# Scan of a bidirectional RWKV-7 layer: both directions' triangular inverses kept in one 64x64 matrix, one factor of each level masked by GpSimd and one by VectorE

## What is computed

```
def step(S, inp):
    r_t, w_t, k_t, v_t, a_t, b_t = inp
    sa = jnp.einsum('zbhvk,zbhk->zbhv', S, a_t)
    S = S * w_t[..., None, :] + sa[..., :, None] * b_t[..., None, :] + v_t[..., :, None] * k_t[..., None, :]
    return S, jnp.einsum('zbhvk,zbhk->zbhv', S, r_t)
_, ys = lax.scan(step, jnp.zeros((2, B, H, N, N), f32), xs)
```

## Time and profile before

| | |
|---|---|
| median of 3 runs | 1307.17 us (1306.04 to 1310.15) |
| the profiled execution's own time | 1311.54 us |
| its span in the trace | 1309.7 us |
| TensorE busy | 96% of the span |
| VectorE, ScalarE, GpSimd busy | 71%, 49%, 34% |
| the scan's eight tiles | from 851.7 us to about 1069 us |

### The profile page before, as it was taken

The page is one execution under the profiler, slowest core; times in us unless marked ns, Lnnn a source line. Parts: engine busy times, 40 slices in busy tenths (PEclk is TensorE's granted clock), DMA queues, the critical chain, the costliest instruction groups (busy, mean ns, idle before and its releaser), DMA issues.

```text
span 1309.7 us, 30302 instructions
## 1 busy us (share of the span) xinstructions
PE 1252.8 (96%) x12608; PEld 1133.1 (87%) x12608; DVE 930.7 (71%) x1334; ACT 645.1 (49%) x1045; POOL 445.1 (34%) x228
## 2 busy tenths in 40 slices
PE   7999999999899999999999799989999998899998
PEld 5799999877889999889999699889989887799998
DVE  7677767686867776766677797686777657766554
ACT  5544446553544455654444466643444333555443
POOL 1244442212134444333444100173343512344442
PEclk9999999999999999999999799899999999999999
DMA  8344555422444555645445444110000014455442
GB/s 342 131 175 181 187 192 182 156 98 97 148 169 179 182 188 192 220 166 187 177 178 184 152 175 152 50 51 4 4 4 4 3 51 157 181 193 188 180 178 111
DMA packets 18667, 188.18 MB, mean 144 GB/s; under 512 B 2064, under 2 KB 2576, under 8 KB 3600
## 3 DMA queue, kind: packets, MB, share of 16 engines
q1 hardware_dynamic: 18576, 186.84, 39.1%
HBM read 185.78 MB, written 1.05 MB: 143 GB/s over the span
## 4 chain that ended last, share of the span: by engine, by line
PE 79%; DVE 13%; ACT 5%; issue 2%; DMA 1%; SPq 0%; DVEq 0%; ACTq 0%
PE gu_bank L257 22%; PE gu_bank L259 11%; PE bank L1382 7%; PE bank L236 7%; PE bank L238 7%; PE bank L237 7%; PE gu_bank L1401 5%; PE gu_bank L236 3%; PE gu_bank L238 3%; PE gu_bank L237 3%; DVE WL L193 2%; PE gu_bank L1382 2%; ACT WH L186 2%; DVE XSQ L407 1%; DVE HX L383 1%
## 5 line engine op out<-in xcount | busy, mean ns | idle before, releaser
L202 POOL TENSOR_TENSOR WL<-raw,WH 128x1024 fp32r<-128x1024 f32 x102 | 341.7, 3351 | 595.8 <-ACT WH L187 574.4
L257 PE MATMUL gu_bank<-HX,WH 128*128 128x512 f32 x1408 | 507.6, 402 | 15.0 <-DVE WL L193 12.4
L259 PE MATMUL gu_bank<-HX,WL 128*128 128x256 f32 x1408 | 397.3, 282 | 0.0
L193 DVE TENSOR_TENSOR WL<-raw,WH 128x2048 fp32r<-128x2048 f32 (+1 forms) x114 | 252.5, 2215 | 135.9 <-ACT WH L186 135.9
L257 PEld LDWEIGHTS gu_bank<-HX,WH 128*128 128x128 f32 x1408 | 266.8, 190 | 81.0 <-DVE WL L193 8.1
L259 PEld LDWEIGHTS gu_bank<-HX,WL 128*128 128x128 f32 x1408 | 268.4, 191 | 0.1
L186 ACT ACTIVATE WH<-raw 128x2048 fp32r<-128x2048 f32 (+1 forms) x114 | 204.6, 1795 | 25.6 <-PE gu_bank L238 13.5
L236 PE MATMUL bank<-PH,WH 128*128 128x256 f32 (+1 forms) x720 | 201.7, 284 | 1.0 <-ACT arena L1939 1.0
L237 PE MATMUL bank<-PL,WH 128*128 128x256 f32 (+1 forms) x720 | 201.6, 283 | 0.0
L238 PE MATMUL bank<-PH,WL 128*128 128x256 f32 (+1 forms) x720 | 201.6, 283 | 0.0
L438 ACT ACTIVATE work<-work 128x256 f32<-128x256 f32 x88 | 36.8, 418 | 279.3 <-DVE work L490 279.3
(11 more groups left out here) (310 smaller groups left out, 1970.5 us busy)
## 6 DMA issues: line engine op xcount, KB each, us to landing
raw<-stream_in SPq DMA_DIRECT2D x114, 1536.0 KB, 6.6
cst<-const_in SPq DMA_DIRECT2D x1, 1568.0 KB, 17.9
X<-xT_in SPq DMA_DIRECT2D x1, 1024.0 KB, 6.1
raw<-stream_in SPq DMA_DIRECT2D x1, 1024.0 KB, 8.1
arena<-hconst_in SPq DMA_DIRECT2D x2, 512.0 KB, 11.5
out<-X SPq DMA_DIRECT2D x4, 256.0 KB, 2.3
arena<-hconst_in SPq DMA_DIRECT2D x1, 768.0 KB, 14.6
arena<-fw_in SPq DMA_DIRECT2D x1, 512.0 KB, 8.9
```

The source lines that it names most:

```text
L193: nc.vector.tensor_tensor(WL[:, slot, :cut], raw[:, slot, :cut], WH[:, slot, :cut].bitcast(fp32), ALU.subtract).then_inc(lo_ready, 1)
L202: (eng or nc.gpsimd).tensor_tensor(WL[:, slot, cut:end], raw[:, slot, cut:end], WH[:, slot, cut:end].bitcast(fp32), ALU.subtract).then_inc ...
L257: nc.tensor.matmul(out[:, :], WH[:, slot, w:w + P], HX[:, x, :, :].rearrange("p i t -> p (i t)"), start=k == 0, stop=False)
L259: return nc.tensor.matmul(out[:, L:2 * L], WL[:, slot, w:w + P], HH[:, x, :], start=False, stop=k == CT - 1)
```

## The change

For each chunk one matrix `SQ` holds z=0's inverse below its diagonal and z=1's above it; the unit diagonal is common. Of the diagonal blocks of width b, the mask `tri` keeps the lower triangle where the block's index is even and the upper one where it is odd. Each level is done once for both directions on full 64x64 matrices: one `zee` and one `update` of 4 calls of `heads`, one copy by ScalarE, one addition by VectorE. For that both factors of a level are first masked: VectorE multiplies `SQ` by `tri` into `VQ` (for `zee`), and GpSimd multiplies the transposed `SW` by `tri` into `WQ` (for `update`). The matrix `GM` with both directions' entries is made by one copy of ScalarE and one predicated copy of VectorE; GpSimd masks it once a level, not twice. At the end VectorE separates the directions into `QF` with two masks, and ScalarE's two copies into `QF` go. The memsets of `ZB` go. TensorE's calls in a level are written in another order.

```diff
-            for z in range(2):
-                act.wait_ge(a_done, 2 * t + z + 1)
-                A(ABD[:, z], z_bank(z), cp).then_inc(abd_ready, 1)
+            act.wait_ge(a_done, 2 * t + 1)
+            if t:
+                act.wait_ge(xl_ready, 5 * t)
+            A(GM, z_bank(0), cp).then_inc(abd_ready, 1)
...
+            def zee(n):
+                pe.wait_ge(xl_ready, 5 * t + n + 1)
+                pe.wait_ge(v_ready, 5 * t + n + 1)
+                for c in range(NCH):
+                    last = heads(ZBANK[0], at64(c), XL[n][:, c], VQ[:, c])
+                last.then_inc(z_done, 1)
+            def update(n):
+                pe.wait_ge(zb_ready, 5 * t + n + 1)
+                if n == 0:
+                    pe.wait_ge(aq_read, 2 * t + 1)
+                pe.wait_ge(w_ready, 5 * t + n + 1)
                 for c in range(NCH):
-                    zb = ZB[n][:, z, c]
-                    zb = side(zb, n, late(z)) if n < len(LEVELS) - 1 else zb.rearrange("p (k b) -> p k b", k=1)
-                    last = side_heads(DBANK[z], P + c * CH // 2, n, TQ[:, z, 0, c], zb)
+                    last = heads(DBANK[0], at64(c), WQ[:, c], ZB[:, c])
                 last.then_inc(d_done, 1)
+            if chunks:
+                pe_r_whole(pe, t - 1, q, 0)
             for n in range(len(LEVELS)):
                 step = chunks and n < NCH
+                zee(n)
                 if step and n:
+                    pe_r_whole(pe, t - 1, q, n)
+                if step and n == 0:
+                    pe_u(pe, t - 1, 0)
+                update(n)
+                if step and n:
+                    pe_u(pe, t - 1, n)
+                if n < 3:
                     pe_tr_wait(pe, t, n)
+                    pe_tr(pe, p, n, range(NCH if n == 0 else NU)).then_inc(tr_done, 1)
                 if step:
                     pe_s(pe, t - 1, q, n)
+                    pe_y(pe, t - 1, q, n)
                 if n == 3:
                     pe.wait_ge(tr_ready, 3 * t + 3)
                     pe_bonus(pe, t)
...
+            def factors(n):
+                dve.wait_ge(t_ready, 6 * t + n + 1)
+                tt(VQ, SQ, mask64("tri", n * CH), ALU.mult).then_inc(v_ready, 1)
+            def turned(n):
+                if t or n:
+                    dve.wait_ge(w_ready, 5 * t + n)
+                nc.vector.transpose(SW.rearrange("p c s -> p (c s)"), SQ.rearrange("p c s -> p (c s)")).then_inc(sw_ready, 1)
+            def put_where(dst, name, off, data):
+                return nc.vector.copy_predicated(dst, mask64(name, off).bitcast(mybir.dt.int32), data)
+            own(tt(SQ, units_of(DBANK[0])[:, :, 0:CH], mask64("first_incl", 0), ALU.mult))
+            dve.wait_ge(aq_done, 2 * t + 2)
+            own.settle()
+            own(put_where(SQ, "first_incl", P, units_of(DBANK[1])[:, :, 0:CH]))
+            own.settle()
+            tt(SQ, SQ, eye, ALU.add).then_inc(t_ready, 1)
+            factors(0)
+            dve.wait_ge(a_done, 2 * t + 2)
+            dve.wait_ge(abd_ready, t + 1)
+            put_where(GM, "strict_incl", 0, z_bank(1)).then_inc(gm_ready, 1)
+            turned(0)
...
+                dve.wait_ge(d_done, 5 * t + n + 1)
+                tt(SQ, SQ, z_bank_of(DBANK[0]), ALU.add).then_inc(t_ready, 1)
+                if n < len(LEVELS) - 1:
+                    factors(n + 1)
+                else:
+                    dve.wait_ge(t_ready, 6 * t + n + 2)
+                    for z in range(2):
+                        tt(QF[:, z * NCH:(z + 1) * NCH, :], SQ, mask64("strict_incl", z * P + CH), ALU.mult).then_inc(qf_ready, 1)
+                if step:
+                    dve_uc(dve, t - 1, n)
+                if n < len(LEVELS) - 1:
+                    turned(n + 1)
...
             for n in range(len(LEVELS)):
-                for z in range(2):
-                    if n == 0:
-                        pool.wait_ge(abd_ready, 2 * t + z + 1)
-                    elif n == 1:
-                        pool.wait_ge(t_ready, 12 * t + 2)
-                    nc.gpsimd.tensor_tensor(XL[n][:, z], ABD[:, z], mask64("level", (z * len(LEVELS) + n) * CH), ALU.mult)\
-                        .then_inc(xl_ready, 1)
+                if n == 0:
+                    pool.wait_ge(gm_ready, t + 1)
+                nc.gpsimd.tensor_tensor(XL[n], GM, mask64("level", n * CH), ALU.mult).then_inc(xl_ready, 1)
+                pool.wait_ge(sw_ready, 5 * t + n + 1)
+                nc.gpsimd.tensor_tensor(WQ, SW, mask64("tri", n * CH), ALU.mult).then_inc(w_ready, 1)
```

More of the change, by code:

```diff
@@ L75 @@
 _cn = [("ones", P), ("ident", P), ("istack", CH), ("blockones", P), ("sel", CT * 16), ("selt", CT * P), ("perm", P),
-       ("first", 2 * CH), ("first_incl", 2 * P), ("strict_incl", 2 * P), ("level", len(LEVELS) * 2 * CH), ("reset", L)]
+       ("first", 2 * CH), ("first_incl", 2 * P), ("strict_incl", 2 * P), ("level", len(LEVELS) * CH), ("tri", len(LEVELS) * CH), ("reset", L)]
 CC = {}
@@ L1386, in both @@
             return AR[p][:, u].rearrange("p i t -> p (i t)")
[L1388 to L1402, removed]
         def at64(n, w=CH):
@@ L1580, in pe_tile @@
                     pe_bonus(pe, t)
-                update(n, 1)
-                if step and n < 3:
-                    pe_y(pe, t - 1, q, n)
                 if not ahead and n in (2, 4):
@@ L1670, in act_tile @@
                     act_high(act, 0)
-            for z in range(2):
-                act.wait_ge(t_ready, 12 * t + 10 + z - 1)
-                keep = side(TQ[:, z, 1].rearrange("p c s -> p (c s)"), len(LEVELS) - 1, 1 - late(z))
-                A(side(QF[:, z * NCH:(z + 1) * NCH, :].rearrange("p c s -> p (c s)"), len(LEVELS) - 1, 1 - late(z)), keep, cp)\
-                    .then_inc(qf_ready, 1)
             if t:
@@ L1769, in units_of @@
                 return b[:, :].rearrange("p (c s) -> p c s", c=NCH)
-            def turned(z, ready):
-                dve.wait_ge(t_ready, ready)
-                nc.vector.transpose(TQ[:, z, 0].rearrange("p c s -> p (c s)"), TQ[:, z, 1].rearrange("p c s -> p (c s)"))\
-                    .then_inc(t0_ready, 1)
-            for z in range(2):
-                dve.wait_ge(aq_done, 2 * t + z + 1)
-                if t:
-                    dve.wait_ge(qf_ready, 2 * t + z - 1)
-                own(tt(TQ[:, z, 1], units_of(DBANK[z])[:, :, 0:CH], mask64("first_incl", z * P), ALU.mult))
-            own.settle()
-            for z in range(2):
-                tt(TQ[:, z, 1], TQ[:, z, 1], eye, ALU.add).then_inc(t_ready, 1)
-            for z in range(2):
-                turned(z, 12 * t + z + 1)
+            def factors(n):
[7 more added lines that the diff above has]
+                return nc.vector.copy_predicated(dst, mask64(name, off).bitcast(mybir.dt.int32), data)
+            if t:
+                dve.wait_ge(qf_ready, 2 * t)
+            dve.wait_ge(aq_done, 2 * t + 1)
+            own(tt(SQ, units_of(DBANK[0])[:, :, 0:CH], mask64("first_incl", 0), ALU.mult))
+            dve.wait_ge(aq_done, 2 * t + 2)
+            own.settle()
+            own(put_where(SQ, "first_incl", P, units_of(DBANK[1])[:, :, 0:CH]))
[6 more added lines that the diff above has]
+            turned(0)
+            if chunks:
+                dve_rc(dve, t - 1, 0)
             for z in range(2):
@@ L2421, in _ @@
             pool.wait_ge(blocks_done, 3 * S_O)
-            for zb in ZB[:-1]:
-                last = nc.gpsimd.memset(zb, 0.0)
-            last.then_inc(zb_clear, 1)
             def pool_step(t, p, c, a):
@@ L2480, in _consts @@
         put("strict_incl", np.concatenate([np.tile(before.T * 1.0, (2, 1)), incl], 1), z * P)
-        for n, b in enumerate(LEVELS):
-            m = (t // (2 * b) == s // (2 * b)) & ((t // b > s // b) if z == 0 else (t // b < s // b))
-            put("level", np.tile(m * 1.0, (2, 1)), (z * len(LEVELS) + n) * CH)
+    for n, b in enumerate(LEVELS):
+        put("level", np.tile(((t // (2 * b) == s // (2 * b)) & (t // b != s // b)) * 1.0, (2, 1)), n * CH)
+        put("tri", np.tile(((t // b == s // b) & np.where(t // b % 2, t <= s, t >= s)) * 1.0, (2, 1)), n * CH)
     put("reset", np.tile((np.arange(L) % CH != 0) * 1.0, (P, 1)))
```

83 lines of the change are left out of this document (21 added, 62 removed).

## The result

The changed kernel takes 1315.57 us (median of 6 runs, 1314.38 to 1319.31), the kernel before, run beside it, 1306.61 us (6 runs, 1305.70 to 1310.15). The ratio is 1.006, with a 95% interval of 1.0041 to 1.0079: slower, by about 9 us. The profiled execution took 1314.38 us.

What follows compares the result with a forecast made beforehand. TensorE's instructions were taken to set the pace. Schedule +4 us and clock +6 made +10: 1321.5 us against the profiled execution's 1311.5, or 1317 against the median, 4.4 lower; range 1301 to 1326 us.

Steps and rivals of the forecast that it cites:

- Removed products: TensorE, five levels: 160 fewer zee and update instructions at 0.029 us each, 4.7 us a tile if nothing replaced them.
- First part: Steady tile up to level 3's first update: 20.9 us becomes 19.7, removed work against 3.5 us of new waits.
- Second part, the step that decides: From level 3's update to the next tile: VectorE's products and GpSimd's operands take turns; 5.9 us becomes 8.1.
- The predicated copy: VectorE's new copy into GM, a cost no row shows: 0.42 us, bounded by 0.2 and 1.15 us.
- Sum of the steady tile: Both parts of a steady tile, less 0.2 us for roundings: 27.6 us against 26.85, +0.75.
- The clock: TensorE's clock falls at six of eight waits; six new 2 us waits at 1.3 us per fall: 6 us.
- PEclk 0.5 in most tiles: Sign that the forecast is right: the profile shows TensorE's clock at half in most tiles.
- a tile of 28.5 us: Sign that the forecast is right: the profile shows a tile taking this long; under 26.9 us would be wrong.
- third rival: Clock falls in every tile, twice in some, with new waits at levels 0 and 3: 1325 us; chance 0.19.
- faster rival: At the tile's end VectorE's four products are not held up: tile 25.5 us, about 1298 us; chance 0.18.

Runs made afterwards that it cites:

- e7: e6 with independent TensorE products, and some VectorE and ScalarE operations, moved into or ahead of TensorE's waits; 1286.82 us, ratio 0.9849.
- e2: The changed kernel with GpSimd's three operand operations on 4 or 2 columns from the second tile on, arithmetic left out; 1309.19 us, ratio 1.0002.
- e8: The changed kernel with GpSimd's three operands replaced by three memsets each from the second tile on; 1307.03 us in one run.
- e1: The changed kernel with VectorE's four dve_alpha products behind the last addition and its masks; 1321.42 us, ratio 1.0088.
- a0: The changed kernel run again, unaltered, for a second profile; 1317.65 us, ratio 1.0078.
- e3: The changed kernel with GpSimd's BSUM moved into level 2 and its first operand ahead of the last level's mask; 1311.08 us, ratio 1.0019.
- e4: The changed kernel with the transposed factor masked by VectorE, not GpSimd; 1310.61 us, ratio 1.0007.
- e6: e4 with one set of the next tile's exponentials moved ahead of ScalarE's transposed copy; 1300.69 us, ratio 0.9948.
- f1: e7 with the transposed factor masked by GpSimd again; 1304.07 us, ratio 0.9961.
- f2: e6 with only the bonus and the mean moved into TensorE's late waits; 1293.06 us, ratio 0.9887.

## Why the prediction was right, and what was off in it

The forecast was 1317 us, slower; it is 1315.6 and 1317.7 us. Step by step:

- *Removed products.* 1280 instructions fewer, as said. (The 5.6 us for 160 in the earlier trace rows are busy time, 0.035 us each, and don't bear out the 0.029; the starts do.) e7 shows a gain of 3.3 us a tile where the waits are small. Not all of it need come from the removed products: before has waits of 1.2 us a tile, and what e7's order would give there was not run.
- *First part.* Forecast 19.7 us; it is 979.21 - 959.59 = 19.62 us in a tile with the clock up. The waits in the brackets, 0.83 us for `ZB` at level 3 and 0.17 + 0.56 + 0.31 = 1.04 in level 0, look shorter than the 1.1 and 1.7 of the forecast. But a bracket starts at an instruction's end, and a group of four, whose starts take 0.12 us, reads as 0.28. By starts, as in the forecast's sum, each wait is 0.16 us longer: 1.0 and 1.5 us. The timeline of TensorE:

```profile
979.21 0.68 PE L1381 MATMUL gu_bank<-scan,scan 64*64 64x64 f32 x16 [0.83 <-ACT scan L1616]
...
1020.96 0.68 PE L1381 MATMUL gu_bank<-scan,scan 64*64 64x64 f32 x16 [0.17 <-ACT scan L1616]
1022.20 0.68 PE L1381 MATMUL bank<-cst,XSQ 64*64 64x64 f32 x16 [0.56 <-DVE scan L1763]
1023.19 0.33 PE L1381 MATMUL bank<-work 64*64 64x64 f32 x4 [0.31 <-DVE arena L1712]
```

- *Second part, the step that decides.* Forecast 8.1, measured 8.14 us. L1836 starts right behind L1856, the four products take 4.18 us, TensorE waits 1.85 (forecast 2). The single-line view of the changed kernel, over all tiles:

```profile
L1697 DVE SCALAR_TENSOR_TENSOR scan<-arena,scan x16: 415/946/1516, 843.9 to 1038.6; 128x256 f32<-128x256 f32 x16
L1702 DVE TENSOR_TENSOR scan<-arena,XSQ x16: 412/1218/1503, 845.7 to 1040.9; 128x256 f32<-128x256 f32 x16
L1740 DVE COPY_PREDICATED scan<-cst,gu_bank x8: 442/444/446, 850.8 to 1044.8; 128x256 f32<-128x256 int32 x8
```

  The medians are 0.95 and 1.22 us, and the four of the tile above took 4.18 / 4 = 1.05 us on average, where 1.2 was forecast. That turns are the cause is shown from both sides: without GpSimd's reads (e2, e8) a product takes 0.42 us, with them and at another time (e1) 0.41. The rule cited from the Trainium skill, "SBUF — State Buffer", section "Who interferes with whom", holds here for two reading operations. It names only GpSimd instructions that read SBUF, and e8 agrees with that: beside memsets, which only write, the products took 0.42 us.
- *The predicated copy.* Forecast 0.42, measured 0.44 us.
- *Sum of the steady tile.* 27.75 us, 0.15 above the 27.6 forecast: 19.62 + 8.13, so the 0.2 taken off for roundings was not there. Tile 0 went from 20.39 to 22.66 us (+2.3, forecast +1; TensorE waits 3.08 us for the last addition ahead of tile 1, where it was 1.93), tile 1 from 31.48 to 31.78, the last one from 30.72 to 28.74 (-2.0, forecast -2.6). All eight together went from 217.2 to 222.8 us in the two profiles: +5.6, where +4 was forecast without falls. Both have falls around tile 1 (two short ones before, at 871 and 881 us, one of about 7 us at 870 in the changed kernel); the one at 925 stands in the changed kernel alone.
- *The clock.* This is the term whose mechanism failed. I took 6 us: a fall at six of eight new waits of 2 us, each worth 1.3 us. But of the eight waits of 1.84 and 1.85 us for the last addition in the two profiles of the changed kernel, the clock fell in one. The first profile has one fall behind tile 1's start, and it isn't at such a wait (windows of 1 us, PEclk third from the end):

```profile
924.00:925.00 1.00, 0.30 (x10) 0.30 (x12) 0.98 (x3) 0.00 (x0) 0.00 (x0) 1.00 0.00 0
925.00:926.00 1.00, 1.00 (x16) 0.74 (x11) 0.42 (x1) 0.00 (x0) 0.93 (x2) 0.66 0.08 16
...
932.00:933.00 1.00, 1.00 (x22) 1.00 (x20) 0.44 (x2) 0.84 (x3) 0.00 (x0) 0.93 0.00 0
```

  It begins at 925, right behind level 3's waits of 0.84 us (to 922.83) and 0.95 us (to 924.70), and lasts 7 us. The slower work fills the time in which TensorE would have waited for the last addition: of the five tile starts between 925 and 1045 only four have the wait of L1769, and the one at 931.54 has none. So the fall costs only 0.9 us here (28.33 and 28.05 us for the two tiles it touches, 27.75 without). In e2, where no such wait is left to fill, it costs 2.7. In a0 the one at the same place makes 28.61 us of 27.75. "PEclk 0.5 in most tiles" and "a tile of 28.5 us" were therefore wrong, and so was the time of the third rival, though it was right to name the waits of level 3. How much of the 9.0 us between the medians is the clock can only be estimated, and roughly, as the falls around tile 1 differ too: the schedule without the fall is 5.6 - 0.9 = 4.7 us in the two profiles, which leaves some 4. The lower mean clock of the changed kernel's runs speaks for this, and so do runs with the same 0.982: 1314.96 us against 1309.85 to 1312.97 for before, a difference of 2.0 to 5.1. By this estimate the forecast took the schedule 0.7 too small and the clock some 2 too large; that the total came so near is in part luck. The kernel in the Trainium skill, "TensorE: Matmul & The Clock Gate", section "HAM oscillation — how this bites in real kernels", has the clock put down in every round, by waits of some 3 to 5 us by that page; here the waits are shorter, and the clock fell in one to three of six rounds.
- *The rivals.* The faster one rested on the products not being held up; e2 and e8 make just this true, and the tile is then 25.85 us where 25.5 was worked out. But the kernel doesn't become faster by it, 1309 in place of 1298 us, since three tiles lose 2.7 us each by the clock. What I missed is that the faster rival keeps the waits of level 3, and has no slack behind them.

What stays open: why the clock falls behind the pair of waits in level 3 in some tiles and not in others, with the waits reading the same (three of six tiles in e2, one of six in each profile of the changed kernel); and where the rest of the clock's 4 us lies, since the profile of before is itself 4.9 us above its median and no faster run of it was traced.

## What to carry to other kernels

Work taken from the busiest engine is worth what is left after the waits that its going uncovers: lay out the chain of one round and look for independent work to write into each wait before judging the edit. Here 4.7 us a tile were removed, and 0.9 lost; with the same products in another order, and one mask on another engine, 3.3 were gained. Where VectorE and GpSimd both have a queue of SBUF-to-SBUF operations, look at when the two queues meet, not at their busy shares; and once the waits on TensorE come in pairs, count them, since the clock may fall behind short ones.

## What the hardware showed that was not expected

- The granted clock fell from 1.00 to 0.50 behind two waits of 0.84 and 0.95 us less than 2 us apart, with no longer one near (e2 at 922, and in e3, e4 and e8 at the same place of the program), and stayed there for about 7 us. Counted over the seven profiles with this pair (the changed kernel twice, e1 to e4, e8), a fall stands behind 15 of 42 pairs, and never behind two in a row; in the four without its first wait (e6, e7, f1, f2; e6 alone keeps the second), at none of 24 such places.
- Neither did it fall in each long wait: the four of 1.84 and 1.85 us in the changed kernel's first profile, such as the one at 957.7 to 959.6, left it at 1.00.
- VectorE's products and GpSimd's memsets, both on SBUF, ran side by side, VectorE's at 0.42 us each; with GpSimd's products in place of the memsets VectorE's took 0.9 to 1.2. One of e8's two theories had expected this.
